# Attention values with the value rows stationary, the probabilities normalised before their transposes, and attention steps in the order scores, transposes, values

## The chip, the cores and the metric

The kernel runs on one core of one Trainium2 chip. The metric is the device time of one execution in microseconds (us), the median of several runs. A core has a matrix engine (PE, its weight loads are shown as PEld), a vector engine (DVE), a scalar engine (ACT), a general engine (POOL) and a queue processor that starts transfers (SP). They run in parallel, each through its own list of instructions in order, and wait for one another through semaphores.

## What is computed

One decoder layer over 256 tokens of width 1024, in float32. Of it the change touches the attention (8 heads of width 64; with 256 tokens there is one block, so the selected blocks are all masked out and causal attention over the own block is left) and the depthwise convolution:

```python
def reference(x, ...):
    h = rmsnorm(x, g_mix[l])
    proj = h @ w_in[l]                       # q, k, v, u (convolution), two gates
    o = moba_attention(q, k, v)              # softmax(q k^T / 8, causal) v, per head
    branch_a = o.reshape(b, s, ATTN_WIDTH) @ w_attn_up[l]
    z = a * jax.nn.sigmoid(g)                # a, g: the halves of u
    z = conv(z, w_dw) + b_dw                 # 31 taps, causal, per channel (512 channels)
    cz = silu(layernorm(z, ln_g, ln_b))
    branch_c = cz @ w_conv_pw[l] + b_conv_pw[l]
    x = x + (gate_a * branch_a + gate_c * branch_c) @ w_out[l]
    h = rmsnorm(x, g_ffn[l])
    x = x + jnp.square(jax.nn.relu(h @ w_ff1[l])) @ w_ff2[l]
    return rmsnorm(x, g_final)
```

## The kernel before

Every large product is computed in split precision: a weight block `raw` (128 x 4 x 512) is split into `w_hi` (a cast on ACT, `high(n)`, L386) and `w_lo` (a subtraction on DVE, `low(n)`, L558), the activations likewise into `a_hi`, `a_lo`, and three matmuls (L811, L812, L815) take the place of one. The work goes in **units**, numbered n: one unit is 4 blocks of rows times 2 token tiles times 3 matmuls of 512 columns, 24 in all. Units 0 to 17 are the input projection, two units to an output block of 512 columns (b = n // 2), which goes to PSUM banks 0 and 1 or 2 and 3 in turn and is taken out by ACT in `take(b)` (L423). So unit 14, the first of block 7, cannot start before `take(5)` has emptied its banks (semaphore `evac`). Units 18 to 25 are the two branches and the output projection, then follow the feed-forward units and a loop over them.

The steps of the attention and of the convolution stand between these units, written out by hand: the loop over n says for each engine what it does at **step n**. Each engine keeps to this order, and a step that waits holds up all that stands behind it on its engine. Weights are prepared three units ahead: step n has `high(n + 3)` first on ACT and `low(n + 3)` on DVE.

Attention goes by pairs of heads, p = 0 to 3, and starts at `S_ATT` = 9. A pair passes through these pieces:

- `scores(p)` on PE, step 9 + p (L873 with the two heads in the upper and the lower 64 rows of the array, L876 adds the causal mask by a matmul with an identity), to banks 6 and 7. It covers 256 query rows as s = 1 (256 keys) and s = 0 (128 keys).
- `row_max(p)` on DVE, same step (L602, L604, L607), then `exps(p)` on ACT (L434, L437), which also sums the rows.
- `probs_transposed(p)` on PE, step 10 + p: six transposes (L798) to banks 4 and 5, copied out by `probs_out(p)` on ACT (L447).
- `values(p)` on PE, step 11 + p (L903): the transposed probabilities are the stationary operand (128 x 128) and 64 columns of `v_nat` the moving one, six float32 matmuls, each of which the trace shows as two. The result goes to banks 6 and 7, columns 384 to 511, beside the next scores.
- `inverse(p)` (L611) and `o_out(p)` (L618) on DVE: the result times the inverse row sums, to `o_nat`, tokens on partitions.
- at step 15 (`S_OT`) eight transposes of `o_nat` on PE (L798), split on ACT and DVE to `b_hi` and `b_lo` (L481, L650).

On PE a step has the order unit, values(n - 11), probs_transposed(n - 10), scores(n - 9). Since scores and values share banks, `scores(p)` waits for `o_made` of the values before:

```python
if p >= 2:
    pe.wait_ge(o_made, p - 1)
```

The convolution is 31 taps for 4 channel blocks, 124 instructions on DVE over z (tap 0: L591, others: L596), dealt out by the table `CONV_AT` as the last piece of steps 2 to 14, after `low(n + 3)`. Step 16 (`S_LN`) has the transposes of the result and the layer norm. At step 13 (`S_BIAS`) ACT splits the bias rows, and POOL then subtracts (L368).

## Time and profile before

| what | us |
|---|---|
| median of 3 runs | 365.58 (365.08 to 365.93) |
| the profiled execution | 366.68 |
| its span on the core | 364.7 |
| PE busy | 353.4 (97% of the span) |
| DVE busy | 256.2 (70%) |
| ACT busy | 174.8 (48%) |

The span is the time from the first to the last instruction of the profiled execution; the time of that execution is 2.0 us more, which lies around it. Matmuls are pipelined, and the end of one is modelled: a matmul of 512 columns is shown with 0.39 us while the next starts 0.23 us after it. So lengths of work on PE are best read as differences of starts.

### The profile page before, as it was taken

To read this page: it belongs to the slowest core of one execution; us is meant where nothing else is said; L and a number is where in the kernel's file an instruction comes from. 1 tells how busy PE (TensorE), PEld (TensorE's weight loads), DVE (VectorE), ACT (ScalarE), POOL (GpSimd) and SP (SyncE) were. 2 spreads that over 40 slices of the span, in tenths; PEclk is the share of its full clock that TensorE was granted. 3 is DMA by queue.
4 is the path that set the end of the run, shared out by engine and by line. 5 is a ranking of instruction groups with operands and counts; after the bars stand their busy time and mean duration, and the time that the engine had idled before them with its cause. 6 is when DMAs were issued, how large, how long until landed. Compare 5 with 4: busy or idle time off the path is not lost.

```text
span 364.7 us, 4601 instructions
## 1 busy us (share of the span) xinstructions
PE 353.4 (97%) x1760; PEld 292.7 (80%) x1760; DVE 256.2 (70%) x314; ACT 174.8 (48%) x195; POOL 9.2 (3%) x18
## 2 busy tenths in 40 slices
PE   6899999999999999999999999999999999999993
PEld 3688888777788888888888888888888888888882
DVE  0878999898899879993858663747636485463834
ACT  3694545554494646342545643436344263541513
POOL 3000000000012000000000000000000000000000
PEclk9899999999999999999999999999999999999999
DMA  7999374633333463757354493571837628260003
GB/s 269 336 345 324 119 229 132 216 117 115 117 115 116 146 238 136 243 188 261 117 152 157 159 328 130 189 259 35 321 115 226 234 67 279 113 230 0 0 0 115
DMA packets 33993, 63.71 MB, mean 175 GB/s; under 512 B 1178, under 2 KB 5434, under 8 KB 33980
## 3 DMA queue, kind: packets, MB, share of 16 engines
q1 hardware_dynamic: 33676, 63.01, 51.4%
q10 hardware_dynamic: 304, 0.53, 0.4%
q8 instruction: 9, 0.15, 0.2%
q14 instruction: 4, 0.03, 0.0%
HBM read 62.48 MB, written 1.05 MB: 174 GB/s over the span
## 4 chain that ended last, share of the span: by engine, by line
PE 89%; DVE 5%; issue 2%; DMA 2%; ACT 0%; SPq 0%; POOLq 0%; POOL 0%
PE ps L815 20%; PE ps L811 20%; PE ps L812 20%; PE ps L1013 16%; PE ps L1015 8%; PE ps L798 3%; DVE conv L596 2%; DMA raw<-in_w_in_dram 2%; DVE w_lo L558 1%; PE ps L873 1%; PE ps L903 1%; PE ps L876 1%; DVE smax L602 0%; DVE w_lo L575 0%; PE ps L987 0%
## 5 line engine op out<-in xcount | busy, mean ns | idle before, releaser
L811 PE MATMUL ps<-w_hi,a_lo 128*128 128x512 f32 x288 | 114.4, 397 | 3.0 <-DVE a_lo L570 3.0
L815 PE MATMUL ps<-w_lo,a_hi 128*128 128x512 f32 x288 | 113.0, 392 | 0.3 <-DVE w_lo L575 0.3
L812 PE MATMUL ps<-w_hi,a_hi 128*128 128x512 f32 x288 | 112.9, 392 | 0.0
L1013 PE MATMUL ps<-b_both,w_hi 128*128 128x512 f32 x256 | 90.8, 399 | 0.0
L1015 PE MATMUL ps<-b_both,w_lo 128*128 128x256 f32 x256 | 71.9, 281 | 0.0
L386 ACT CAST w_hi<-raw 128x2048 fp32r<-128x2048 f32 (+1 forms) x30 | 56.4, 1884 | 31.3 <-PE ps L815 26.9
L558 DVE TENSOR_TENSOR w_lo<-raw,w_hi 128x2048 fp32r<-128x2048 f32 x29 | 66.1, 2285 | 4.7 <-ACT w_hi L386 4.6
L762 DVE TENSOR_TENSOR w_lo<-raw,w_hi 128x2048 fp32r<-128x2048 f32 x28 | 63.5, 2289 | 6.4 <-ACT w_hi L532 6.4
L811 PEld LDWEIGHTS ps<-w_hi,a_lo 128*128 128x128 f32 x288 | 54.5, 189 | 14.2 <-DVE w_hi L564 3.2
L815 PEld LDWEIGHTS ps<-w_lo,a_hi 128*128 128x128 f32 x288 | 54.5, 189 | 12.5 <-DVE w_lo L575 0.8
L812 PEld LDWEIGHTS ps<-w_hi,a_hi 128*128 128x128 f32 x288 | 54.5, 189 | 10.7
L1013 PEld LDWEIGHTS ps<-b_both,w_hi 128*128 128x128 f32 x256 | 48.1, 188 | 11.9
L532 ACT CAST w_hi<-raw 128x2048 fp32r<-128x2048 f32 x28 | 52.8, 1911 | 7.8 <-PE ps L815 7.8
L596 DVE SCALAR_TENSOR_TENSOR conv<-z,dw,conv 128x256 f32<-128x256 f32 x120 | 50.8, 499 | 0.0
L1015 PEld LDWEIGHTS ps<-b_both,w_lo 128*128 128x128 f32 x256 | 48.3, 189 | 0.3
L741 DVE TENSOR_TENSOR nat<-ps,nat 128x512 f32<-128x512 f32 x16 | 11.1, 692 | 42.5 <-ACT nat L516 42.5
L516 ACT COPY nat<-ps 128x512 f32<-128x512 f32 x16 | 9.4, 588 | 57.5 <-PE ps L1015 57.5
L811 PE MATMUL ps<-w_hi,b_both 128*128 128x512 f32 x48 | 18.9, 393 | 0.0
L815 PE MATMUL ps<-w_lo,b_both 128*128 128x512 f32 x48 | 18.7, 390 | 0.0
L812 PE MATMUL ps<-w_hi,b_both 128*128 128x512 f32 x48 | 18.7, 389 | 0.0
L754 DVE TENSOR_TENSOR a_lo<-nat,a_hi 128x1024 fp32r<-128x1024 f32 x7 | 8.6, 1223 | 14.1 <-ACT a_hi L522 14.1
L522 ACT CAST a_hi<-nat 128x1024 fp32r<-128x1024 f32 x7 | 7.4, 1052 | 21.8 <-PE ps L815 21.6
(109 smaller groups left out, 218.8 us busy)
## 6 DMA issues: line engine op xcount, KB each, us to landing
raw<-in_w_ff_dram SPq DMA_DIRECT2D x32, 1024.0 KB, 5.4
raw<-in_w_in_dram SPq DMA_DIRECT2D x14, 1024.0 KB, 5.3
raw<-in_w_out_dram SPq DMA_DIRECT2D x4, 1024.0 KB, 5.0
raw<-in_w_in_dram SPq DMA_DIRECT2D x6, 512.0 KB, 7.5
raw<-in_w_attn_up_dram SPq DMA_DIRECT2D x2, 1024.0 KB, 5.1
raw<-in_w_conv_pw_dram SPq DMA_DIRECT2D x2, 1024.0 KB, 5.1
res<-in_x_dram SPq DMA_DIRECT2D x2, 512.0 KB, 3.7
raw<-in_w_in_dram SPq DMA_DIRECT2D x4, 256.0 KB, 5.9
```

The lines of the kernel that those rows point to most:

```text
L386: nc.scalar.copy(w_hi[:, n % SLOTS, part], raw[:, n % SLOTS, part]).then_inc(hi_made, 1)
L532: nc.scalar.copy(w_hi[:, slot], raw[:, slot]).then_inc(hi_made, 1)
L558: nc.vector.tensor_tensor(w_lo[:, n % SLOTS], raw[:, n % SLOTS], w_hi[:, n % SLOTS].bitcast(F32), ALU.subtract).then_inc(lo_made, 1)
L596: nc.vector.scalar_tensor_tensor(out=conv[:, c], in0=z[:, c, tap:tap + T], scalar=dw[:, w:w + 1], in1=conv[:, c], op0=ALU.mult, op1=ALU.ad ...
L741: nc.vector.tensor_tensor(hid[:, pair], ps[:, TB + 2 * half:TB + 2 * half + 2, 0:T], hid[:, pair], ALU.add).then_inc(sum_made, 1)
L762: nc.vector.tensor_tensor(w_lo[:, slot], raw[:, slot], w_hi[:, slot].bitcast(F32), ALU.subtract).then_inc(lo_made, 1)
L798: return nc.tensor.transpose(dst, src, ident[0:src.shape[0], 0:src.shape[0]])
L811: nc.tensor.matmul(dst, lo[:, tok], w_hi[:, slot, k], start=start, stop=False)
L812: nc.tensor.matmul(dst, hi[:, tok], w_hi[:, slot, k], start=False, stop=False)
L815: return nc.tensor.matmul(dst, hi[:, tok], w_lo[:, slot, k], start=False, stop=stop)
L1013: nc.tensor.matmul(ps[:, TB + c], w_hi[:, slot, k, cols], b_both[:, kk].rearrange("p a t -> p (a t)"), start=kk == 0, stop=False)
L1015: last = nc.tensor.matmul(ps[:, TB + c, 0:T], w_lo[:, slot, k, cols], b_hi[:, kk], start=False, stop=kk == KD - 1)
```

## The change

The values are computed the other way round: 64 columns of `v_nat` are stationary, and the transposed probabilities move (256 columns for the first 128 keys, 128 for the others; the first 128 queries have no others). The two heads of a pair write to the lower and the upper 64 partitions of one half bank (bank 5, columns 256 to 511), with channels on partitions, which is what the next product needs: the eight transposes of step 15 go, and `o_nat` becomes `o_t`. As the row sums then no longer lie on the partitions, the probabilities are normalised ahead of their transposes, by four instructions on ACT (`normalise`), for which `inverse(p)` moves one step forward on DVE, to behind `low(n + 3)`. `o_out` becomes a copy on ACT. The mask matmul of s = 1 covers only the 128 keys that need it. On PE a step has the order unit, scores, transposes, values; `scores(p)` waits for the exponentials of the pair before and no longer for the values. Tap 0 of the convolution goes to ACT (4 instructions, steps 2 and 4), and `CONV_AT` gives DVE 11 or 12 taps in steps 9 to 12, where it had 10, and 9 and 1 in steps 13 and 14, where it had 10 and 9. The bias split moves to step 14.

```diff
 S_QT, S_KT = 6, 8
 S_ATT = 9
 PAIRS = HEADS // 2
-S_OT = S_ATT + 6
-S_BIAS = 13
+S_OLO = S_ATT + 6
+S_BIAS = 14
 S_LN = 16
 S_SILU = U_ATTN
 
 
-CONV = [(tap, c) for tap in range(10) for c in (0, 1)]
-CONV += [(tap, c) for tap in range(10) for c in (2, 3)]
+CONV = [(tap, c) for tap in range(1, 10) for c in (0, 1)]
+CONV += [(tap, c) for tap in range(1, 10) for c in (2, 3)]
 CONV += [(tap, c) for tap in range(10, TAPS) for c in range(4)]
-CONV_AT = {2: 6, 3: 14, 4: 9, 5: 9, 6: 9, 7: 9, 8: 9, 9: 10, 10: 10, 11: 10, 12: 10, 13: 10, 14: 9}
-assert len(CONV) == sum(CONV_AT.values()) == TAPS * 4
+CONV_AT = {2: 6, 3: 12, 4: 9, 5: 9, 6: 9, 7: 9, 8: 9, 9: 11, 10: 12, 11: 12, 12: 12, 13: 9, 14: 1}
+assert len(CONV) == sum(CONV_AT.values()) == (TAPS - 1) * 4
 
...
+            def normalise(p):
+
+                act.wait_ge(rinv_made, p + 1)
+                act.wait_ge(exp_made, p + 1)
+                for h in range(2):
+                    part = probs[:, 256 * h:256 * h + 256]
+                    nc.scalar.activation(part, part, ACT.Copy, scale=rinv[:, p, h:h + 1])
+                for h in range(2):
+                    part = probs[:, 512 + 128 * h:640 + 128 * h]
+                    last = nc.scalar.activation(part, part, ACT.Copy, scale=rinv[:, p, 2 + h:3 + h])
+                last.then_inc(norm_made, 1)
+
+            def o_out(p):
+
+                act.wait_ge(pv_done, p + 1)
+                nc.scalar.copy(o_t[:, p], o_pair()).then_inc(ot_made, 1)
+
...
@@ -459,6 +481,12 @@
                         act.wait_ge(glu_tr, c + 1)
                         nc.scalar.activation(conv[:, c], ps[:, TB + c, T:2 * T], ACT.Sigmoid,
                                              bias=vec[:, V_BGLU + CC + c:V_BGLU + CC + c + 1]).then_inc(glu_sig, 1)
+                    act.wait_ge(vec_made, 2)
+                    act.wait_ge(const_made, 4)
+                    for c in (2 * GLU_AT[n], 2 * GLU_AT[n] + 1):
+                        act.wait_ge(z_made, c + 1)
+                        nc.scalar.activation(conv[:, c], z[:, c, 0:T], ACT.Identity, scale=dw[:, c:c + 1],
+                                             bias=vec[:, V_BDW + c:V_BDW + c + 1]).then_inc(conv_first, 1)
...
+                if S_ATT + 2 <= n < S_ATT + 2 + PAIRS:
+                    o_out(n - S_ATT - 2)
                 if S_ATT + 1 <= n <= S_ATT + PAIRS:
                     probs_out(n - S_ATT - 1)
                 if S_ATT <= n < S_ATT + PAIRS:
                     exps(n - S_ATT)
+                    normalise(n - S_ATT)
...
-                if n == S_OT:
-                    act.wait_ge(o_tr, 1)
-                    nc.scalar.copy(b_hi[:, 0:CC], chunks(TB)).then_inc(o_hi, 1)
+                if n == S_OLO:
+                    act.wait_ge(ot_made, PAIRS)
+                    nc.scalar.copy(b_hi[:, 0:CC], o_t[:]).then_inc(o_hi, 1)
...
                 for m in conv_share(step):
                     tap, c = CONV[m]
-                    if tap == 0:
-                        nc.vector.tensor_scalar(conv[:, c], z[:, c, 0:T], dw[:, c:c + 1], vec[:, V_BDW + c:V_BDW + c + 1],
-                                                ALU.mult, ALU.add).then_inc(conv_step, 1)
+                    if tap == 1:
+                        dve.wait_ge(conv_first, c + 1)
                     else:
                         dve.wait_ge(conv_step, conv_before(m) + 1)
-                        w = tap * CC + c
-                        nc.vector.scalar_tensor_tensor(out=conv[:, c], in0=z[:, c, tap:tap + T], scalar=dw[:, w:w + 1],
-                                                       in1=conv[:, c], op0=ALU.mult, op1=ALU.add).then_inc(conv_step, 1)
+                    w = tap * CC + c
+                    nc.vector.scalar_tensor_tensor(out=conv[:, c], in0=z[:, c, tap:tap + T], scalar=dw[:, w:w + 1],
+                                                   in1=conv[:, c], op0=ALU.mult, op1=ALU.add).then_inc(conv_step, 1)
...
             def inverse(p):
                 dve.wait_ge(exp_made, p + 1)
                 nc.vector.reciprocal(rinv[:, p], psums[:, p]).then_inc(rinv_made, 1)
-
-            def o_out(p):
-
-                dve.wait_ge(pv_done, p + 1)
-                dve.wait_ge(rinv_made, p + 1)
-                for s in range(2):
-                    last = nc.vector.tensor_tensor(
-                        o_nat[:, 1 - s, 128 * p:128 * p + 128].rearrange("p (h d) -> p h d", h=2),
-                        ps[:, SB0:SB0 + 2, 384 + HD * s:384 + HD * s + HD],
-                        rinv[:, p, 2 * s:2 * s + 2].rearrange("p (h a) -> p h a", a=1).to_broadcast([P, 2, HD]), ALU.mult)
-                last.then_inc(o_made, 1)
...
-                if S_ATT + 2 <= n < S_ATT + 2 + PAIRS:
-                    o_out(n - S_ATT - 2)
-                if S_ATT + 1 <= n < S_ATT + 1 + PAIRS:
-                    inverse(n - S_ATT - 1)
                 if S_ATT <= n < S_ATT + PAIRS:
                     row_max(n - S_ATT)
-                if n == S_OT:
-                    dve.wait_ge(o_hi, 1)
-                    nc.vector.tensor_tensor(b_lo[:, 0:CC], chunks(TB), b_hi[:, 0:CC].bitcast(F32),
-                                            ALU.subtract).then_inc(o_lo, 1)
...
                 if n + AHEAD < U_LOOP + AHEAD_LOOP:
                     low(n + AHEAD)
+                if S_ATT <= n < S_ATT + PAIRS:
+                    inverse(n - S_ATT)
                 conv_products(n)
+                if n == S_OLO:
+                    dve.wait_ge(o_hi, 1)
+                    nc.vector.tensor_tensor(b_lo[:, 0:CC], o_t[:], b_hi[:, 0:CC].bitcast(F32),
+                                            ALU.subtract).then_inc(o_lo, 1)
...
             def scores(p):
 
-
-
-                if p >= 2:
-                    pe.wait_ge(o_made, p - 1)
                 for s, at, keys in ((1, 0, 256), (0, 256, 128)):
...
                     for h in range(2):
-                        last = nc.tensor.matmul(ps[:, SB0 + h, at:at + keys], ident_b[:], mask_b[:, T - keys:T],
+                        last = nc.tensor.matmul(ps[:, SB0 + h, at + keys - P:at + keys], ident_b[:], mask_b[:, P:T],
                                                 start=False, stop=True)
...
             def probs_transposed(p):
-                pe.wait_ge(exp_made, p + 1)
+                pe.wait_ge(norm_made, p + 1)
                 if p:
                     pe.wait_ge(pt_made, p)
-                for blk in range(6):
-                    o = blk * P
-                    last = transpose(ps[:, TB + o // W, o % W:o % W + P], probs[:, o:o + P])
+                if p > 1:
+                    pe.wait_ge(ot_made, p - 1)
+                for h in range(2):
+                    for blk, at in enumerate((512 + P * h, 256 * h, 256 * h + P)):
+                        o = (3 * h + blk) * P
+                        last = transpose(ps[:, TB + o // W, o % W:o % W + P], probs[:, at:at + P])
                 last.then_inc(p_tr, 1)
 
             def values(p):
 
                 pe.wait_ge(pt_made, p + 1)
                 if p:
-                    pe.wait_ge(o_made, p)
-                if p + 2 <= PAIRS:
-                    pe.wait_ge(exp_made, p + 2)
-                for s in range(2):
+                    pe.wait_ge(ot_made, p)
+                for kb in range(2):
                     for h in range(2):
                         head = slice(HD * (2 * p + h), HD * (2 * p + h) + HD)
-                        o = 384 + HD * s
-                        n_keys = 2 - s
-                        for kb in range(n_keys):
-                            at = 256 * h + P * kb if s == 0 else 512 + P * h
-                            last = nc.tensor.matmul(ps[:, SB0 + h, o:o + HD], probs_t[:, at:at + P], v_nat[:, kb, head],
-                                                    start=kb == 0, stop=kb == n_keys - 1)
+                        at = 3 * h * P + 2 * P * kb
+                        last = nc.tensor.matmul(o_pair()[HD * h:HD * h + HD, kb * P:T], v_nat[:, kb, head],
+                                                probs_t[:, at:at + T - kb * P], start=kb == 0, stop=kb == 1)
                 last.then_inc(pv_done, 1)
 
             def glu_transposed(hb):
@@ -933,24 +944,23 @@
                 if n == S_KT:
                     pe.wait_ge(evac, K + 1)
                     transpose_chunks(SB0, lambda t, c: nat[:, t, W + c * P:W + c * P + P]).then_inc(qk_tr, 1)
+                if S_ATT <= n < S_ATT + PAIRS:
+                    if n == S_ATT:
+                        pe.wait_ge(qk_made, 2)
+                        pe.wait_ge(ident_made, 3)
+                    else:
+                        pe.wait_ge(exp_made, n - S_ATT)
+                    scores(n - S_ATT)
+                if S_ATT + 1 <= n <= S_ATT + PAIRS:
+                    probs_transposed(n - S_ATT - 1)
                 if S_ATT + 2 <= n < S_ATT + 2 + PAIRS:
                     if n == S_ATT + 2:
                         pe.wait_ge(evac, V + 1)
                     values(n - S_ATT - 2)
-                if S_ATT + 1 <= n <= S_ATT + PAIRS:
-                    probs_transposed(n - S_ATT - 1)
-                if S_ATT <= n < S_ATT + PAIRS:
-                    if n == S_ATT:
-                        pe.wait_ge(qk_made, 2)
-                        pe.wait_ge(ident_made, 3)
-                    scores(n - S_ATT)
-                if n == S_OT:
-                    pe.wait_ge(o_made, PAIRS)
-                    transpose_chunks(TB, lambda t, c: o_nat[:, t, c * P:c * P + P]).then_inc(o_tr, 1)
...
-                    pe.wait_ge(conv_step, TAPS * CC)
-                    pe.wait_ge(o_lo, 1)
+                    pe.wait_ge(conv_step, (TAPS - 1) * CC)
+                    pe.wait_ge(ot_made, PAIRS)
```

On **PE**, step 12 (behind unit 12) stands before:

```order
L903 MATMUL ps<-v_nat,probs_t 128x64 x6
L798 MATMUL ps<-ident,probs 128x128 x6
L873 MATMUL ps<-qk_t 128x256 x2
L876 MATMUL ps<-mask_b,ident_b 128x256 x2
L873 MATMUL ps<-qk_t 128x128 x2
L876 MATMUL ps<-mask_b,ident_b 128x128 x2
L811 MATMUL ps<-w_hi,a_lo 128x512
```

and step 12 now:

```order
L886 MATMUL ps<-qk_t 128x256 x2
L889 MATMUL ps<-mask_b,ident_b 128x128 x2
L886 MATMUL ps<-qk_t 128x128 x2
L889 MATMUL ps<-mask_b,ident_b 128x128 x2
L815 MATMUL ps<-ident,probs 128x128 x6
L914 MATMUL ps<-probs_t,v_nat 64x256 x2
L914 MATMUL ps<-probs_t,v_nat 64x128 x2
L828 MATMUL ps<-w_hi,a_lo 128x512
```

The rows ahead of the last, which is the start of unit 13, are the pieces of pairs 1 to 3. Values moved from the front to the back, from six matmuls of 64 columns to two of 256 and two of 128 (the 64 is the width of the stationary operand), and the first mask has 128 columns in place of 256.

On **ACT**, from the exponentials of pair 3 (step 12) to the cast of unit 16's weights, stands before:

```order
L434 ACTIVATE probs,psums<-ps,nbias 128x256 x2
L437 ACTIVATE probs,psums<-ps,nbias 128x128 x2
L423 ACT_TABLE_LOAD
L423 ACTIVATE gates<-ps,rstd 128x512 x2
L386 CAST w_hi<-raw 128x2048
L468 CAST bias_rows<-gfin_bc 128x1024
```

and now:

```order
L439 ACTIVATE probs,psums<-ps,nbias 128x256 x2
L442 ACTIVATE probs,psums<-ps,nbias 128x128 x2
L453 ACTIVATE probs<-probs,rinv 128x256 x2
L456 ACTIVATE probs<-probs,rinv 128x128 x2
L428 ACT_TABLE_LOAD
L428 ACTIVATE gates<-ps,rstd 128x512 x2
L391 CAST w_hi<-raw 128x2048
L462 COPY o_t<-ps 128x256
L469 COPY probs_t<-ps 128x768
```

Four multiplications (`probs<-probs,rinv`) moved in ahead of the table load and of `take(5)` (`gates<-ps,rstd`), the copy of the values stands ahead of `probs_out(3)`, and the bias rows have gone from here.

On **DVE**, step 12 stands before:

```order
L618 TENSOR_TENSOR o_nat<-ps,rinv 128x128 x2
L611 RECIPROCAL rinv<-psums 128x4
L602 TENSOR_REDUCE smax<-ps 128x2
L604 TENSOR_REDUCE smax<-ps 128x2
L607 TENSOR_SCALAR nbias<-smax 128x4
L558 TENSOR_TENSOR w_lo<-raw,w_hi 128x2048
L596 SCALAR_TENSOR_TENSOR conv<-z,dw,conv 128x256 x10
```

and now:

```order
L632 TENSOR_REDUCE smax<-ps 128x2
L634 TENSOR_REDUCE smax<-ps 128x2
L637 TENSOR_SCALAR nbias<-smax 128x4
L589 TENSOR_TENSOR w_lo<-raw,w_hi 128x2048
L641 RECIPROCAL rinv<-psums 128x4
L626 SCALAR_TENSOR_TENSOR conv<-z,dw,conv 128x256 x12
```

The copy of the values is gone, the reciprocal moved from ahead of the row maxima to behind the subtraction `w_lo`, now for the pair of the same step, and 12 taps stand where 10 stood.

## Rows read from the trace of the kernel before

**Rows 1.** The page, part 1 (busy time, instructions) and part 4 (chain that ended last).

```profile
PE 353.4 (97%) x1760; PEld 292.7 (80%) x1760; DVE 256.2 (70%) x314; ACT 174.8 (48%) x195; POOL 9.2 (3%) x18
PE 89%; DVE 5%; issue 2%; DMA 2%; ACT 0%; SPq 0%; POOLq 0%; POOL 0%
```

**Rows 2.** Windows: length, busy of PE, PEld, DVE, ACT, POOL, clock, DMA.

```profile
60.00:130.00 70.00, 69.22 (x374) 56.28 (x374) 62.24 (x118) 39.20 (x61) 4.63 (x2) 1.00 0.42 140
200.00:300.00 100.00, 100.00 (x502) 84.50 (x501) 58.74 (x39) 44.98 (x33) 0.00 (x0) 1.00 0.57 187
```

**Rows 3.** Timeline of PE, step 12: start, length, what, [idle before <-releaser].

```profile
95.15 0.39 PE L815 MATMUL ps<-w_lo,a_hi 128*128 128x512 f32 x1
95.38 1.44 PE L903 MATMUL ps<-v_nat,probs_t 128*128 128x64 f32 x12
96.66 0.82 PE L798 MATMUL ps<-ident,probs 128*128 128x128 f32 x6
97.87 0.70 PE L873 MATMUL ps<-qk_t 64*128 64x256 f32 x4 [0.39 <-DVE o_nat L618]
98.51 0.39 PE L876 MATMUL ps<-mask_b,ident_b 128*128 128x256 bf16 x2
98.83 0.49 PE L873 MATMUL ps<-qk_t 64*128 64x128 f32 x4
99.25 0.29 PE L876 MATMUL ps<-mask_b,ident_b 128*128 128x128 bf16 x2
99.35 0.48 PE L811 MATMUL ps<-w_hi,a_lo 128*128 128x512 f32 x1
```

**Rows 4.** Timeline of PE: values of pair 2, its next transposes, unit 14.

```profile
104.89 1.45 PE L903 MATMUL ps<-v_nat,probs_t 128*128 128x64 f32 x12
106.17 0.82 PE L798 MATMUL ps<-ident,probs 128*128 128x128 f32 x6
106.75 0.47 PE L811 MATMUL ps<-w_hi,a_lo 128*128 128x512 f32 x1
```

**Rows 5.** Timeline of PE: output transposes of step 15, unit 16.

```profile
119.14 1.04 PE L798 MATMUL ps<-ident,o_nat 128*128 128x128 f32 x8
119.93 0.47 PE L811 MATMUL ps<-w_hi,a_lo 128*128 128x512 f32 x1
```

**Rows 6.** Groups by line and form: count, then busy us, mean ns, idle before.

```profile
L876 PE MATMUL ps<-mask_b,ident_b 128*128 128x256 bf16 x8 | 1.6, 278 | 0.0
L876 PE MATMUL ps<-mask_b,ident_b 128*128 128x128 bf16 x8 | 1.1, 224 | 0.0
L434 ACT ACTIVATE probs<-ps,nbias 128x256 f32<-128x256 f32 x8 | 3.7, 471 | 7.4 <-DVE nbias L607 7.4
L437 ACT ACTIVATE probs<-ps,nbias 128x128 f32<-128x128 f32 x8 | 2.9, 368 | 0.0
L548 ACT ACTIVATE res<-gates,rstd 128x512 f32<-128x512 f32 x2 | 1.4, 724 | 1.7 <-POOL rstd L363 1.7
```

**Rows 7.** Timeline of DVE, step 12 and the taps of step 13.

```profile
99.58 0.69 DVE L602 TENSOR_REDUCE smax<-ps 128x2 f32<-128x512 f32 x1 [1.68 <-PE ps L876]
100.71 2.28 DVE L558 TENSOR_TENSOR w_lo<-raw,w_hi 128x2048 fp32r<-128x2048 f32 x1
102.91 4.04 DVE L596 SCALAR_TENSOR_TENSOR conv<-z,dw,conv 128x256 f32<-128x256 f32 x10
106.87 0.48 DVE L618 TENSOR_TENSOR o_nat<-ps,rinv 128x128 f32<-128x128 f32 x2
109.53 6.20 DVE L596 SCALAR_TENSOR_TENSOR conv<-z,dw,conv 128x256 f32<-128x256 f32 x10
```

**Rows 8.** Timeline of ACT, step 12: first exponential, table load, `take(5)`.

```profile
100.84 0.48 ACT L434 ACTIVATE probs<-ps,nbias 128x256 f32<-128x256 f32 x1 [2.52 <-DVE nbias L607]
102.57 1.28 ACT L423 ACT_TABLE_LOAD   x1
105.03 1.90 ACT L386 CAST w_hi<-raw 128x2048 fp32r<-128x2048 f32 x1
```

More of the change, by code:

```diff
@@ L81, in conv_before @@
     tap, c = CONV[m]
-    return CONV.index((tap - 1, c))
+    return CONV.index((tap - 1, c)) if tap > 1 else None
 def build(nc, x, g_mix, w_in, b_glu, w_dw, b_dw, ln_g, ln_b, w_conv_pw, b_conv_pw,
@@ L225, in build @@
         z_made = sem("z_made")
+        conv_first = sem("conv_first")
         conv_step = sem("conv_step")
@@ L245, in build @@
         rinv_made = sem("rinv_made")
-        o_made = sem("o_made")
-        o_tr = sem("o_tr")
+        norm_made = sem("norm_made")
+        ot_made = sem("ot_made")
         o_hi = sem("o_hi")
```

12 lines of the change are left out of this document (7 added, 5 removed).

## The prediction

> **What bounds the kernel now.** The page comes first: PE is busy for 353.4 of 364.7 us, and the chain that ended last runs 89% over PE [rows 1]. Then the windows: in the stretch that holds the attention, 60 to 130, PE is busy for 69.22 of 70 us and DVE for 62.24, and in the feed-forward stretch 200 to 300 PE is busy for 100 of 100 [rows 2]. So PE is the bound everywhere from 60 on, and what the change is worth is the PE time it takes out between the units, less every wait that it brings in. What comes later has no idle PE time that could swallow a gain (it depends on PE, and moves forward with it), so a gain at unit 17 is a gain at the end. DVE, at 89% of the attention stretch, is the engine to watch: the change also moves work there. Third, the timeline of PE at step 12, which is the model for steps 11 and 12 [rows 3]: the last matmul of unit 12 starts at 95.15 and holds PE for 0.23, then values take 1.28 (95.38 to 96.66), transposes and a wait 1.21 (to 97.87), scores 1.48 (to 99.35). All that is 3.97 between two units. A unit is 5.54 (99.35 to the next values at 104.89) [rows 3, 4].
>
> **The four gains on PE.** I take each from differences of starts.
>
> Output transposes: the eight of step 15 take 0.79 (119.14 to 119.93) [rows 5]. They go, and nothing takes their place on PE: **0.79**.
>
> Masks: eight mask matmuls of 256 columns become 128 wide. Mean lengths are 278 and 224 ns [rows 6], so 8 x 0.054 = **0.43**. Scores then take 1.48 - 0.11 = 1.37.
>
> Waits: six transposes alone take 0.58 (106.17 to 106.75) [rows 4], or 0.10 each by the eight above, so of the 1.21 about 0.60 is work and 0.61 is the wait of the scores for `o_made`; the view's idle column has 0.39, because ends are modelled [rows 3]. Step 11 has the same wait. The new scores wait for exponentials that are long done (below), so 2 x 0.6 = **1.2**, with 0.8 as the low end.
>
> Values: now 12 instructions in 1.28 [rows 3]. The new form isn't in this trace; the nearest rows are the scores, where the two heads also share the array, by rows in place of columns. There the 256-column pair takes 0.64 (97.87 to 98.51) and the 128-column pair 0.42 (98.83 to 99.25), each as four shown matmuls. The difference, 0.22 for two passes that do 128 columns less, gives 0.11 for a pass of 128 and 0.22 for one of 256, if both heads run at once, and an overhead of 0.20 for entering and leaving. (In turn, the 256-column pair would need at least 4 x 0.22 = 0.88, and it took 0.64, so for scores they do run at once.) New values are one such pair of 256 and one of 128, next to each other: 0.44 + 0.22 + 0.20 = 0.86. If the overhead is paid twice, 1.06; with none, 0.66. If heads in different columns run in turn, 4 x 0.22 + 4 x 0.11 + 0.20 = 1.52. I take 0.90, near the one-overhead value, since nothing else stands between the two pairs: 4 x (1.28 - 0.90) = **1.52**, with ends of 4 x (1.28 - 0.66) = 2.5 and 4 x (1.28 - 1.52) = -0.96.
>
> The trace shows two heads at once only for row halves. The Trainium skill (TensorEngine Tiling (Array Packing), Performance Considerations) advises just this swap for 64 columns, with two column tiles, for a factor of up to 2; the same page says under Tiling Modes that a change of mode drains the engine, which speaks against one more kind of matmul in each step. The first rule would put the values at the 0.86 above in place of 1.52; for the second the 0.20 of the score rows is the price, already in.
>
> Sum of the gains: 0.79 + 0.43 + 1.2 + 1.52 = **3.94**.
>
> **What the change adds, and who waits.** I set a clock to zero at the end of the scores of pair 0, the start of unit 10, and add rows.
>
> PE: unit 10 to 5.54; scores and transposes 1.97, so unit 11 from 7.51 to 13.05; scores, transposes, values 2.87, so unit 12 from 15.92 to 21.46; again 2.87, so unit 13 from 24.33 to 29.87; transposes and values 1.50, so PE wants unit 14 at **31.37**.
>
> DVE: the maxima start 0.23 behind the end of the scores (99.58 against 99.35) [rows 3, 7]. A step is maxima 1.13, `low` 2.20, reciprocal 0.1, and taps at 0.396 (10 in 102.91 to 106.87) [rows 7]: 7.79 with 11 taps, 8.18 with 12. So the maxima of pairs 1, 2, 3 start at 8.02, 16.20, 24.38. Their scores are done at 6.9, 14.4 and 22.8: it is now the taps that make DVE late, by about 1.3. In rows 7 DVE had 1.68 idle in their place. At 8.18 against PE's 8.41 per step the lag doesn't grow.
>
> ACT: exponentials start 1.26 behind the maxima (99.58 to 100.84) and take 1.6 [rows 7, 8]. The normalisation waits for the reciprocal, which stands behind `low`: 3.33 + 0.2 after the maxima. Its price, from both sides: ACT reading SBUF with a scale from a tile took 724 ns for 512 columns, and 128 columns are worth 0.10 (471 - 368) [rows 6], so 0.52 and 0.42; ACT instructions follow one another 0.1 before the shown end, so 2 x 0.42 + 2 x 0.32 = 1.48. If SBUF cost nothing over PSUM it would be 1.3; I keep 1.9 as the high end.
>
> Now each wait. Scores of pair 3 (21.46) need the exponentials of pair 2: 16.20 + 2.9 + 0.1 = 19.2, in time. Transposes of pair 2 (22.83) need its normalisation: 16.20 + 3.53 + 1.48 + 0.1 = 21.3, in time. Transposes of pair 3 (29.87): 24.38 + 5.11 = 29.5, in time by 0.4. **Unit 14** needs `take(5)`, which stands behind the normalisation of pair 3: 29.4, then table load and evacuation 2.46 (102.57 to 105.03) [rows 8], so 31.85, and 0.1 for the signal: 31.95, against 31.37. PE waits **0.6**. Before, `take(5)` ended at 105.03, 1.7 before unit 14 (106.75) [rows 4, 8]; this cover is gone. With normalisation at 1.3 the wait is 0.4, at 1.9 it is 1.0 (part of it ahead of the transposes).
>
> Edits at no cost: four first taps on ACT (about 1.1 in each of steps 2 and 4) and the copy of the values (0.3 to 0.4) lie in ACT's slack (ACT busy 48% [rows 1]), and what they delay is a weight cast prepared three units ahead. The moved bias split makes POOL work beside `low(17)` instead of beside taps. It was there that ten taps took 6.20 and not 4.04 [rows 7], so DVE may lose 2.2 in step 14 too. But after the maxima of pair 3 it has left 12, 9 and 1 taps and two `low`: 24.38 + 8.18 + 2.2 + 3.6 + 2.2 + 2.2 + 0.4 = 43.2, and PE wants the last tap only at the end of unit 16, at 31.95 + 3 x 5.54 + 0.9 = 49.5. Each wait instruction more is some tens of ns on a sequencer that runs ahead.
>
> **Forecast.** 3.94 - 0.6 = 3.3 to 3.4. I take 3.4: the profiled execution of 366.68 (span 364.7 and 2.0 around it) would become 363.3 (span 361.3). That execution was 1.1 above the median, so the median of 365.58 becomes **362.2**.
>
> **Rivals.**
> (a) The two heads run in turn, so the change of form doesn't do what it should. Then values take 1.52. The gain is 0.79 + 0.43 + 1.2 - 0.96 = 1.46, and the wait at unit 14 is gone, since PE comes 1.9 later than in the sum above: **364.1**. For it: the trace has no column halves. Against it: the row halves do run at once. In between (half overlapped, 1.1 to 1.2): gain 2.6 to 2.9.
> (b) DVE becomes the bound in steps 10 to 12, mildly: taps at 0.50 instead of 0.396 make its step 9.4 against 8.4, the lag grows by 1.0 a step, and the waits take 3.0 of the 3.9: gain 0.9, and at 0.52 nothing measurable is left: **365.2**.
> (c) The other side: the taps run at 0.62, as the ten from 109.53 did [rows 7]. If ACT's normalisation from SBUF to SBUF slows them as POOL's work did there, a DVE step is 10.9 against 8.4. The spare time of exponentials (2.2) and transposes (1.5 and 0.4) is used up in the first such step; PE then waits 0.45 and 0.8 in step 12, about 3.9 before the transposes of pair 3 and 1.0 before unit 14, some 6.1 in all, against 3.94 gained: 2.1 slower, **367.7**. It decides from about 0.54 a tap. Against it: casts from SBUF to SBUF on ACT stand in this stretch too, and the taps beside the one at 105.03 are among the ten of 4.04 [rows 7, 8].
>
> **How the numbers follow.** Forecast, with values of 0.7 to 1.1 and a wait of 0.3 to 1.2 (gain 2.8 to 3.9): 0.68. (a), with half overlaps down to a gain of 1.2: 0.21. (b), within 0.2%: 0.06. (c): 0.04; a cause I haven't seen gives the last 0.01. A measurement of this kernel can tell about 0.2%, 0.7 us. The range goes from 361.3 (gain of 3.9 and 0.4 for scatter) to 364.4 (case (a) and 0.3 of scatter). Faster 0.90, same 0.06, slower 0.04.
>
> **What the profile after would show.** Right: unit 12 to unit 13 (start to start) 8.4 instead of 9.5; two new value groups of 256 and 128 columns with start pairs a few ns apart, 0.9 in all; no idle before the scores; unit 15 to unit 16 without transposes, 5.5 instead of 6.3; DVE maxima starting 1 to 1.6 behind the scores, with no idle before them; one wait of about 0.6 at unit 14, released by `take(5)`. Wrong: value matmuls of the two heads each starting when the other ends (a); taps of over 0.45, and waits of transposes for the normalisation in steps 11 to 13 (b, c); a wait at unit 16 or 17, or a feed-forward stretch in which PE is less than fully busy, where I count on none.

## The result and the profile after

| | before | after |
|---|---|---|
| median | 365.62 us (365.08 to 366.34, 6 runs) | 362.38 us (361.91 to 363.14, 6 runs) |
| the profiled execution | 366.68 | 362.36 |
| its span | 364.7 | 360.4 |

The ratio of the times is 0.9911, with a 95% interval from 0.99 to 0.9921: 3.2 us faster, where 3.4 were forecast.

The page of after, its parts 1 and 4, answers to [rows 1]. PE is busy 3.8 us less at the same 97%, and ACT 9.1 us more.

```profile
PE 349.6 (97%) x1736; PEld 287.0 (80%) x1736; DVE 253.2 (70%) x302; ACT 183.9 (51%) x219; POOL 10.6 (3%) x18
...
PE 90%; ACT 2%; DMA 2%; issue 2%; SPq 2%; DVE 0%; POOLq 0%; POOL 0%; ACTq 0%
```

The windows answer to [rows 2] (length, busy of PE, PEld, DVE, ACT, POOL, clock, DMA share, GB/s).

```profile
60.00:130.00 70.00, 70.00 (x366) 54.68 (x365) 63.17 (x110) 47.68 (x82) 6.07 (x2) 1.00 0.42 143
200.00:300.00 100.00, 100.00 (x500) 84.50 (x499) 59.71 (x37) 44.46 (x32) 0.00 (x0) 1.00 0.57 189
```

The view shows no idle time of PE between 60 and 130 any more, and the feed-forward stretch is as full as before. So the gain of the attention steps went through to the end.

The timeline of PE at step 12 answers to [rows 3].

```profile
93.14 0.39 PE L832 MATMUL ps<-w_lo,a_hi 128*128 128x512 f32 x1
93.45 0.70 PE L886 MATMUL ps<-qk_t 64*128 64x256 f32 x4
94.09 0.29 PE L889 MATMUL ps<-mask_b,ident_b 128*128 128x128 bf16 x2
94.31 0.49 PE L886 MATMUL ps<-qk_t 64*128 64x128 f32 x4
94.73 0.29 PE L889 MATMUL ps<-mask_b,ident_b 128*128 128x128 bf16 x2
94.85 0.82 PE L815 MATMUL ps<-ident,probs 128*128 128x128 f32 x6
95.61 0.87 PE L914 MATMUL ps<-probs_t,v_nat 128*64 128x256 f32 x8
96.41 0.50 PE L828 MATMUL ps<-w_hi,a_lo 128*128 128x512 f32 x1
96.74 0.39 PE L829 MATMUL ps<-w_hi,a_hi 128*128 128x512 f32 x1
```

Nothing waits. Scores take 1.40 (93.45 to 94.85), transposes 0.76, values 0.80. One row is not what it was: the last matmul of unit 12 holds PE for 0.31 (93.14 to 93.45), not 0.23. And unit 13's first takes 0.33 (96.41 to 96.74). These edges come back below.

The length of a step, from the first matmul of its unit to the first of the next, follows from such rows (step 12: 87.77 to 96.41 after). In us:

| step | 9 | 10 | 11 | 12 | 13 | 14 | 15 | 16 | sum |
|---|---|---|---|---|---|---|---|---|---|
| before | 7.11 | 7.79 | 9.54 | 9.54 | 7.40 | 6.81 | 6.37 | 6.33 | 60.89 |
| after | 7.00 | 7.63 | 8.58 | 8.63 | 7.18 | 6.48 | 5.61 | 6.23 | 57.35 |
| gain | 0.11 | 0.16 | 0.96 | 0.91 | 0.22 | 0.33 | 0.76 | 0.10 | 3.54 |
| predicted | 0.11 | 0.11 | 1.10 | 1.10 | -0.22 | 0.38 | 0.79 | 0 | 3.4 |

From the start of unit 17 to that of unit 25 it is 47.25 us before and 47.26 after. The two profiled executions differ by a further 0.8 us ahead of unit 9 (it starts at 65.37 and at 64.56). The edits of steps 2 to 4 aren't the cause: over all the kernels of this study unit 9 starts between 64.04 and 65.69, at 64.11 in the one that has the new steps 9 to 16 with the taps of before, and the medians don't show this part.

The same starts can be summed by kind of work over steps 9 to 16, which closes the account: the values fell from 5.10 to 3.24 (1.86), the scores with their masks from 5.91 to 5.56 (0.35), the transposes with the waits behind them from 5.34 to 3.62 (1.72), and the matmuls of the units rose from 44.54 to 44.92 (-0.38). That is 3.55.

### The profile page after: what moved, and what is told of

Its sections match the earlier page's. It is cut to its first block, busy times and chain, and to the rows that moved or that the text cites. A ratio compares the mean times of both kernels' runs of the same rounds, so it can differ in the third digit from the quotient of the medians.

```text
span 360.4 us, 4567 instructions
## 1 busy us (share of the span) xinstructions
PE 349.6 (97%) x1736; PEld 287.0 (80%) x1736; DVE 253.2 (70%) x302; ACT 183.9 (51%) x219; POOL 10.6 (3%) x18
## 4 chain that ended last, share of the span: by engine, by line
PE 90%; ACT 2%; DMA 2%; issue 2%; SPq 2%; DVE 0%; POOLq 0%; POOL 0%; ACTq 0%
PE ps L828 20%; PE ps L832 19%; PE ps L829 19%; PE ps L1023 17%; PE ps L1025 8%; PE ps L815 3%; DMA raw<-in_w_in_dram 2%; PE ps L886 1%; ACT w_hi L391 1%; SPq L301 1%; PE ps L914 1%; SPq L316 1%; PE ps L889 0%; ACT nat L410 0%; ACT nat L428 0%
```

## The experiments

"Steps" below means the sum of steps 9 to 16 as in this table. The kernels ran on three chips in three groups, with before beside each group at 365.73, 365.72 and 365.71.

**Do the two heads of the values run at once? Two runs.** In after the two heads' matmuls alternate. The first run groups them by head; the second starts from the first.

```diff
-                for kb in range(2):
-                    for h in range(2):
+                for h in range(2):
+                    for kb in range(2):
```

> The kernel after, with one edit: the loops of the values are exchanged, so that each head has its 256-column and its 128-column matmul in a row, and only then comes the other head. In the kernel after the group of values takes 0.80 us (start to the next unit). Theory A, the two column halves run at once because matmuls of different heads stand next to each other: now they meet only at the border, the group takes 1.3 to 1.5, the kernel is 4 x 0.6 = 2.0 to 2.8 us slower (364.4 to 365.2), and the small wait at unit 14 stays small. Rival B, the order within the group does not matter, since the engine overlaps what it may, or since the short time of the group has another cause than overlap: 0.8 as before, no change within 0.3 us.

It took 362.15 (361.92 to 362.43), ratio 0.9902 [0.9885, 0.9919], steps 57.40: B was right and my theory A wrong. The timeline of PE between 86.46 and 86.50 shows why:

```profile
86.45 0.44 PE L914 MATMUL ps<-probs_t,v_nat 128*64 128x256 f32 x2
```

Within 0.05 us two matmuls of 256 columns have started. Each head has one of these, which the trace shows as two, and head 1's is issued after all of head 0's, those of 128 columns too. So the two column halves are fed out of the order of the program (the second run shows below that the pair isn't the two parts of one head's matmul), and the order inside the group is worth nothing. That leaves open whether they run at once because of the halves. Second run:

```diff
-o_pair()[HD * h:HD * h + HD, kb * P:T]
+o_pair()[0:HD, kb * P:T]
```

> The kernel with the values grouped by head (as in e1_heads_apart, 0.81 us for the group), in which both heads write to the same 64 output partitions, so the upper half of the values is not computed and the lower one holds only the second head. Same number and size of matmuls. Theory A, the 0.80 us are two heads at once in different column halves, whatever order they are issued in: in one half they run in turn, the group takes 4 x 0.22 + 4 x 0.11 + 0.2 or a little less, 1.35 to 1.5, and the kernel is 4 x 0.6 = 2.2 to 2.8 us slower than e1 (364.4 to 364.9), with starts of the two heads no longer in pairs. Rival B, 64-column stationary operands are simply that fast: 0.8, no change.

It took 364.83 (364.19 to 367.18), ratio 0.9978 [0.9956, 0.9999], steps 59.80: 2.40 over the first run, 0.6 in each step with values. Both heads now write the lower 64 partitions, and the upper half of the values isn't computed. The group of values, of the first run and then of this one:

```profile
86.45 0.88 PE L914 MATMUL ps<-probs_t,v_nat 128*64 128x256 f32 x8
```

```profile
87.58 1.51 PE L914 MATMUL ps<-probs_t,v_nat 128*64 128x256 f32 x8
```

And the timeline of this run between 87.59 and 87.63:

```profile
87.58 0.43 PE L914 MATMUL ps<-probs_t,v_nat 128*64 128x256 f32 x1
```

Same instructions, 0.63 longer, and of 256 columns only one starts in the same 0.05 us. The concurrency of the halves is 2.4 us of this kernel: without it the kernel would have taken about 364.8, 0.7 above rival (a)'s 364.1. One thing stays open: in this run the two heads share their destination as well as their half, and the runs don't tell which of the two makes them take turns.

**What is the order worth, without the new form?** Before, with the order scores, transposes, values on PE, and ACT and DVE doing their parts in the order that this needs. The values keep their old form and go to bank 5. The edit on PE:

```diff
-                    values(n - S_ATT - 2)
...
                     scores(n - S_ATT)
...
                     probs_transposed(n - S_ATT - 1)
...
+                    values(n - S_ATT - 2)
```

> The kernel before with the order of the steps alone: scores, transposes, values on PE, and values in their old form (six matmuls of 64 columns) but written to bank 5, so that scores need not wait for them. DVE copies them out behind its weight subtraction, ACT copies the transposes behind the exponentials. Masks, taps, output transposes as before. Theory A, of the 3.2 us of the whole change about 0.9 is the wait that the order removes: transposes and wait were 1.21 in steps 11 and 12 and become 0.75, twice 0.46, less 0.17 in step 13, so 0.6 to 1.1 us faster than before (364.5 to 365.0), with no idle PE time ahead of the scores. Rival B, the order gives nothing alone, since transposes or values then wait for the slower copy on DVE: within 0.3 us of before, and new waits at transposes or values.

It took 364.9 (364.44 to 365.16), ratio 0.9975 [0.9964, 0.9986], steps 59.99, 0.90 less: A. Steps 11 and 12 gave 0.49 and 0.45, step 10 gave 0.06, and steps 13 and 14 took 0.11 back. No row of its timeline of PE has an idle column in these steps. Of step 12:

```profile
95.80 0.82 PE L800 MATMUL ps<-ident,probs 128*128 128x128 f32 x6
96.46 1.45 PE L903 MATMUL ps<-v_nat,probs_t 128*128 128x64 f32 x12
```

The transposes take 0.66 here. So the wait taken out was worth about 0.45 a step, in two steps, and not 0.6. The trace of before could have told this: its step 10 has the same two groups with no wait between them, and there the transposes ahead of scores take 0.75, so of the 1.21 of step 12 only 0.46 was a wait.

```profile
78.04 0.81 PE L798 MATMUL ps<-ident,probs 128*128 128x128 f32 x6
78.79 0.70 PE L873 MATMUL ps<-qk_t 64*128 64x256 f32 x4
```

**The narrower mask alone.**

```diff
-last = nc.tensor.matmul(ps[:, SB0 + h, at:at + keys], ident_b[:], mask_b[:, T - keys:T],
+last = nc.tensor.matmul(ps[:, SB0 + h, at + keys - P:at + keys], ident_b[:], mask_b[:, P:T],
```

> The kernel before with one edit: the mask matmul of s = 1 covers 128 keys and not 256. Theory A (the scores of after take 1.40 and those of before 1.48, so 0.08 a step): steps 9 to 12 each 0.08 shorter, 0.32 in all, ratio 0.9991. The prediction's term (lengths of the two forms, 0.054 a matmul): 0.11 a step, 0.43 in all. Rival B: the bf16 mask matmuls hide behind the score matmuls, and the 0.08 of after comes from what stands around the scores there: nothing in steps 9 and 10, and steps 11 and 12 unchanged too.

Steps 9 to 12 took 7.00, 7.68, 9.43 and 9.43, each 0.11 less, 0.43 in all; 365.31 (364.8 to 365.7), ratio 0.9988 [0.9979, 0.9997]. The prediction's term was right to the hundredth, and my revision of it to 0.32 wrong. Its timeline:

```profile
96.71 0.70 PE L873 MATMUL ps<-qk_t 64*128 64x256 f32 x4 [0.38 <-DVE o_nat L618]
...
97.98 0.29 PE L876 MATMUL ps<-mask_b,ident_b 128*128 128x128 bf16 x2
98.08 0.48 PE L811 MATMUL ps<-w_hi,a_lo 128*128 128x512 f32 x1
```

Scores take 1.37 (96.71 to 98.08), as predicted. The 1.40 of after has 0.03 more behind its masks (94.73 to 94.85 against 97.98 to 98.08), where transposes follow and not a unit: an edge again.

**Fewer changes of the array's shape.** The two masks of a head are merged into one of 384 columns, put first, and the row halves of the scores follow without a break. (The mask tile grows to 384 columns; that part of the edit isn't shown.)

```diff
+                for h in range(2):
+                    nc.tensor.matmul(ps[:, SB0 + h, 0:384], ident_b[:], mask_b[:], start=True, stop=False)
                 for s, at, keys in ((1, 0, 256), (0, 256, 128)):
...
-                    for h in range(2):
-                        last = nc.tensor.matmul(ps[:, SB0 + h, at + keys - P:at + keys], ident_b[:], mask_b[:, P:T],
```

> The kernel after with the masks of a head as one matmul of 384 columns (zeros, triangle, triangle) ahead of both score matmuls, which then accumulate onto it: one entry to the 64-row form per pair instead of two. Theory A on the price of an entry: the group of scores falls from 1.40 to 1.15 to 1.25 us (0.20 less for an entry, 0.11 more mask columns, weight loads of the masks hidden behind the unit). Theory B on what of it arrives: the maxima of pair 3 hang on the taps and not on the scores, so only the saving of pair 0 (0.2) moves take(5), and unit 14 now waits 0.5 to 0.6: the kernel gains only 0.2 to 0.3 (362.1). Rival, nothing hangs on DVE's chain: the whole 0.6 to 0.9 arrives (361.6), and unit 14 does not wait.

It took 361.81 (361.61 to 362.04), ratio 0.9892 [0.9876, 0.9909], steps 56.96: 0.39 less than after, in between what was expected. Steps 9 to 12 gained 0.18, 0.10, 0.15 and 0.15, at and below the low end of the 0.15 to 0.25 expected, and step 13 lost 0.21 to a wait. Its timeline of PE at step 12, and then unit 14:

```profile
92.56 0.50 PE L886 MATMUL ps<-mask_b,ident_b 128*128 128x384 bf16 x2
92.99 0.92 PE L890 MATMUL ps<-qk_t 64*128 64x256 f32 x8
93.84 0.87 PE L817 MATMUL ps<-ident,probs 128*128 128x128 f32 x6
94.64 0.87 PE L915 MATMUL ps<-probs_t,v_nat 128*64 128x256 f32 x8
...
102.84 0.50 PE L830 MATMUL ps<-w_hi,a_lo 128*128 128x512 f32 x1 [0.18 <-ACT gates L430]
```

Masks and scores take 1.28 (92.56 to 93.84) and the transposes 0.80. The matmul of unit 12 ahead of the masks, which use the full array, takes 0.23 again and not 0.31. PE comes to unit 14 earlier, and `take(5)` is late there, as the prediction had reckoned for after itself.

**The convolution's shares, four runs.** More taps in steps 10 to 12, so that DVE is later behind the scores:

```diff
-9: 11, 10: 12, 11: 12, 12: 12, 13: 9, 14: 1}
+9: 11, 10: 14, 11: 14, 12: 14, 13: 3, 14: 1}
```

> The kernel after with 14 taps in place of 12 in steps 10, 11 and 12 and 3 in place of 9 in step 13 (120 in all). Theory A, DVE is late by the taps, and the chain maxima, exponentials, reciprocal, normalisation, table load, take(5) is just in time for unit 14 (a wait of 0.04): two steps with two more taps each move the maxima of pair 3 by 4 x 0.395 = 1.6 us, and all of it arrives: about 0.6 ahead of the transposes of pair 3 and 0.9 ahead of unit 14, the kernel 1.4 to 1.7 us slower (363.8 to 364.1). Rival B, the chain has slack that the trace does not show or the taps merely fill DVE's idle time: slower by less than 0.5.

It took 363.61 (363.52 to 363.71), ratio 0.994 [0.9924, 0.9957], a little below A's 363.8 to 364.1. Only step 13 grew, from 7.18 to 8.67, by 1.49 where 1.4 to 1.7 were expected:

```profile
102.14 0.87 PE L815 MATMUL ps<-ident,probs 128*128 128x128 f32 x6 [0.34 <-ACT probs L456]
...
104.72 0.50 PE L828 MATMUL ps<-w_hi,a_lo 128*128 128x512 f32 x1 [0.90 <-ACT gates L428]
```

This is the chain of rivals (b) and (c): DVE late, normalisation late, then transposes and `take(5)`. It is real and decides where the prediction put it, in step 13. Now the shares of before, with the first tap still on ACT (the same table was then put on the kernel with the mask first), and then with all 124 taps on DVE (table and first taps then as in before). The edit of the first of these two:

```diff
-9: 11, 10: 12, 11: 12, 12: 12, 13: 9, 14: 1}
+9: 10, 10: 10, 11: 10, 12: 10, 13: 10, 14: 7}
```

> The kernel after with 10 taps in each of steps 9 to 13 and 7 in step 14 (120 in all), as the steps had before. Theory A, the chain over DVE and ACT is just in time with 12 taps, so with fewer it comes early and PE, which waited only 0.04, gains nothing: within 0.2 us of the kernel after (362.1 to 362.5), DVE idle ahead of the maxima again by 1 to 1.7 us, take(5) ending 1.3 to 2 earlier relative to unit 14. The larger shares then are no part of the gain. Rival B, the larger shares are worth something, since 10 and 7 taps in steps 13 and 14, where POOL slows them, make the taps late for step 16: 0.5 or more slower, with PE waiting ahead of the convolution's transposes.

> After, with the first tap back on DVE and the convolution shares of before (124 taps on DVE, none on ACT). Theory A (first taps on ACT and the larger shares are no part of the gain, since DVE is late behind the scores only by what the waits can spare): the length of after within 0.2, steps 9 to 13 within 0.05 of it, unit 14 with a wait of at most 0.1. Rival B (ACT's help is needed): the four taps more on DVE make it late in steps 13 to 16, and unit 16 or 17 waits 0.5 to 1.6 for conv or w_lo.

They took 362.03 (361.99 to 362.74), ratio 0.9903 [0.9885, 0.9921], and 362.29 (361.8 to 362.82), ratio 0.9912 [0.9897, 0.9927], with steps 57.34 and 57.37 against 57.35. Neither the larger shares nor ACT's taps are a part of the gain. But one thing expected of the first didn't come: `take(5)` was to end 1.3 to 2 us earlier against unit 14. DVE's maxima of pair 3 do start earlier, 1.35 ahead of unit 13 (94.79 against 96.14) where after has 0.58 (95.83 against 96.41), yet the table load starts 4.56 behind unit 13 in both. Two rows of its timelines, of ACT and of DVE, show why:

```profile
96.26 0.37 ACT L462 COPY o_t<-ps 128x256 f32<-128x256 f32 x1 [2.39 <-PE ps L914]
98.98 0.18 DVE L641 RECIPROCAL rinv<-psums 128x4 f32<-128x4 f32 x1 [0.77 <-ACT probs L442]
```

On ACT the exponentials of pair 3 stand behind the copies of the values and of the transposes, and these wait for PE's values of the same step. So a second chain leads to `take(5)`, which starts at PE's values and moves with PE. It leaves unit 14 a wait of 0.04 (the group of values ahead of it takes 0.84, the other groups 0.80), however early DVE is. In after the chain over DVE's taps and `w_lo` ends together with it, at the reciprocal of pair 3 (99.25); with 14 taps it ends later, and decides. The shares matter only where PE comes to unit 14 earlier:

> Both together: masks of 384 columns first (e4_mask_first, which saved 0.15 to 0.18 a step and lost 0.21 of it again at unit 14) and 10 taps a step. Theory A, the 0.21 at unit 14 was DVE's lag by the taps: it goes, and steps 9 to 13 are each 0.10 to 0.18 shorter than in the kernel after, 0.6 in all over steps 9 to 16, 361.6 us, 0.2 faster than e4_mask_first. Rival B, the wait at unit 14 has another cause (the table load and take(5) alone): it stays at 0.2 and the kernel equals e4_mask_first (361.8).

It took 361.36 (361.31 to 362.93), ratio 0.9879 [0.9862, 0.9895], steps 56.80. The wait at unit 14 is back at the 0.04 of after (step 13 is 7.18 and not 7.39, step 14 gives 0.05 back), and this kernel has the lowest median of the study, though its interval overlaps that of the mask first alone.

**The other order with the new form, two runs.** After, with the order values, transposes, scores. As the result of the values shares a bank with the transposes, these then wait for ACT's copy `o_t`.

```diff
+                    values(n - S_ATT - 2)
...
                     probs_transposed(n - S_ATT - 1)
...
-                    values(n - S_ATT - 2)
...
             def probs_transposed(p):
-                if p > 1:
-                    pe.wait_ge(ot_made, p - 1)
+                if p:
+                    pe.wait_ge(ot_made, p)
```

> The kernel after with the steps on PE in the old order values, transposes, scores. Values and transposes share bank 5, so the transposes have to wait for the copy of the values just done (in the kernel after that copy has a whole unit of time). Theory A, the order is worth a bank wait per step in the new form too: 0.6 to 0.8 ahead of the transposes in steps 11, 12 and 13, and up to 0.3 at unit 14, together 1.9 to 2.6 us slower than the kernel after (364.2 to 364.9). Rival B, the order does not matter once values have left the banks of the scores: within 0.3 us of the kernel after.

It took 369.67 (369.17 to 370.37), ratio 1.0102 [1.0082, 1.0122], steps 64.54: 7.2 more than after, where 1.9 to 2.6 were expected. I had missed what stands ahead of the copy on ACT. Timeline of PE, the transposes of steps 12 and 13, and unit 14:

```profile
97.13 0.85 PE L815 MATMUL ps<-ident,probs 128*128 128x128 f32 x6 [0.97 <-ACT o_t L462]
...
109.33 0.85 PE L815 MATMUL ps<-ident,probs 128*128 128x128 f32 x6 [3.55 <-ACT o_t L462]
...
110.75 0.63 PE L828 MATMUL ps<-w_hi,a_lo 128*128 128x512 f32 x1
111.18 0.63 PE L829 MATMUL ps<-w_hi,a_hi 128*128 128x512 f32 x1
```

And its timeline of ACT ahead of the second of these waits:

```profile
104.57 1.28 ACT L428 ACT_TABLE_LOAD   x1
105.86 1.26 ACT L428 ACTIVATE gates<-ps,rstd 128x512 f32<-128x512 f32 x2
107.02 1.90 ACT L391 CAST w_hi<-raw 128x2048 fp32r<-128x2048 f32 x1
108.81 0.38 ACT L462 COPY o_t<-ps 128x256 f32<-128x256 f32 x1
```

The values were issued at 104.91, and their copy stood behind a table load, `take(5)` and a weight cast until 108.81. Behind the 3.55 us of idle PE the clock fell, though not at once: PE worked for 1.4 us at the upper level first (its transposes and three matmuls of unit 14), and from 110.75 on matmuls of 512 columns start 0.43 apart and not 0.23. The windows give 0.66 as the granted clock of that stretch (second last columns: clock, then DMA share):

```profile
105.00:110.00 5.00, 1.45 (x15) 1.09 (x15) 3.79 (x8) 4.18 (x5) 0.00 (x0) 1.00 0.48 186
110.00:115.00 5.00, 5.00 (x17) 3.97 (x16) 5.00 (x11) 4.70 (x5) 0.01 (x1) 0.66 0.42 156
```

That is a part of the stretch at the lower of the two levels (1.2 GHz) and the rest at the upper (2.4 GHz). Step 14 took 8.07 for it and not 6.48, another 1.6 us. To tell ACT's queue from the order itself, ACT then copies first:

```diff
+                if S_ATT + 2 <= n < S_ATT + 2 + PAIRS:
+                    o_out(n - S_ATT - 2)
                 if n + AHEAD < U_LOOP + AHEAD_LOOP:
                     high(n + AHEAD)
...
-                if S_ATT + 2 <= n < S_ATT + 2 + PAIRS:
-                    o_out(n - S_ATT - 2)
```

> After with the PE order of before (values, transposes, scores; transposes wait for the copy of the values), as in e6_old_order, but ACT copies the values ahead of the weight cast, not behind it. Theory A (the 7.2 us lost in e6_old_order are waits for a copy queued behind casts on ACT, plus a fall of the clock behind the longest): PE idle about 0.7 in steps 11 and 12 and 1.7 to 1.9 in step 13, no fall of the clock, 3.1 to 3.3 slower than after, about 365.4. Rival B (the order and the shared bank cost this in themselves, whatever ACT's order): as e6_old_order, 369 to 370.

It took 365.15 (364.67 to 366.03), ratio 0.9985 [0.9976, 0.9995], steps 60.29, 2.94 more than after: A, a little below its 3.1 to 3.3. The waits:

```profile
95.08 0.85 PE L815 MATMUL ps<-ident,probs 128*128 128x128 f32 x6 [0.56 <-ACT o_t L462]
...
105.48 0.85 PE L815 MATMUL ps<-ident,probs 128*128 128x128 f32 x6 [1.72 <-ACT o_t L462]
106.08 0.48 PE L828 MATMUL ps<-w_hi,a_lo 128*128 128x512 f32 x1
106.40 0.40 PE L829 MATMUL ps<-w_hi,a_hi 128*128 128x512 f32 x1
```

After 1.72 idle the clock stays up: the matmuls behind 106.40 start 0.23 apart. So 4.3 of the 7.2 were the place of one copy on ACT (waits and clock), and 2.9 the order with a shared bank.

## Why the prediction was right, and where its steps were off

The bound was right: PE, from 60 on, and each gain went through to the end. Of the sum:

**Output transposes**, 0.79: step 15 gave 0.76, and unit 16 another 0.10 that wasn't in the sum. Behind the eight transposes its first matmul held PE for 0.32; now it follows unit 15 directly and takes 0.23 (115.68 to 115.91). Rows of PE's timeline of after, against [rows 5]:

```profile
115.68 0.39 PE L828 MATMUL ps<-w_hi,a_lo 128*128 128x512 f32 x1
115.91 0.39 PE L829 MATMUL ps<-w_hi,a_hi 128*128 128x512 f32 x1
```

**Masks**, 0.43: measured alone, 0.43.

**Values**, 0.90 taken, 0.80 measured (95.61 to 96.41, and 109.27 to 110.07): 4 x 0.48 = 1.92 and not 1.52. The reasoning from the row halves held: both heads at once and one overhead gave 0.86, and heads in turn gave 1.52, where the run with both in one half has 1.44. The first passes of the two heads start within 0.01 us in after (86.97 to 86.98).

The advice of the Trainium skill (TensorEngine Tiling (Array Packing), Performance Considerations) to swap the operands for 64 columns and use two column tiles, which the prediction weighed, agrees with the group's sizes here: 0.80 in two halves, 0.63 more in one.

**Waits**, 1.2 taken, about 0.9 measured. This is the mis-sized term. The step that failed reads "six transposes alone take 0.58", so that about 0.60 of the 1.21 is work. That 0.58 was a group with a unit behind it. With values behind it, it takes 0.75 (timeline of after):

```profile
102.00 0.82 PE L815 MATMUL ps<-ident,probs 128*128 128x128 f32 x6
102.75 0.87 PE L914 MATMUL ps<-probs_t,v_nat 128*64 128x256 f32 x8
```

With scores behind it, it takes 0.75 too, and with the old values behind it 0.66. So what follows starts later, most of all where it uses halves of the array; the old values use the whole of it, so a change of shape isn't all of the price. The idle column of [rows 3], 0.39, was closer to the truth than the 0.61 that I put in its place; 0.46 is what remained. The prediction had put the price of a change of the array's shape inside the group, as its 0.20. A part of it lies in the neighbours: 0.08 in the last matmul of a unit ahead of scores or new values (0.31 against 0.23) and 0.17 in the transposes ahead of either (0.75 against 0.58). The first matmul of a unit takes 0.31 behind any small group, halves or not, against 0.23 behind another unit, and 0.33 behind the new values. With the values coming out 0.1 cheaper, steps 11 and 12 gave 0.96 and 0.91, not 1.10.

**Unit 14**, a wait of 0.6 taken, 0.04 measured; this cost term was the largest single miss. ACT's side came out right in time: its timeline in step 12 has

```profile
99.46 0.91 ACT L453 ACTIVATE probs<-probs,rinv 128x256 f32<-128x256 f32 x2 [0.24 <-DVE rinv L641]
...
100.97 1.28 ACT L428 ACT_TABLE_LOAD   x1
102.27 1.26 ACT L428 ACTIVATE gates<-ps,rstd 128x512 f32<-128x512 f32 x2
103.42 1.90 ACT L391 CAST w_hi<-raw 128x2048 fp32r<-128x2048 f32 x1
```

1.51 for the normalisation (99.46 to 100.97, 1.48 reckoned) and 2.45 for load and evacuation. The exponentials started 1.65 behind the maxima (97.48 against 95.83) and not 1.26, for the reason that the run with 10 taps showed; the prediction had left ACT's copies out. It cost nothing, since the subtraction `w_lo` on DVE ended no sooner. But PE came later than on my clock. Steps 10 to 13 without waits were reckoned at 7.51, 8.41, 8.41 and 7.04 and took 7.63, 8.58, 8.63 and 7.14, 0.6 more in all, which is these edges. The same error took 0.4 out of the gains of these steps (2.29 for 2.69) and took away the wait of 0.6, so the sum of 3.4 stands close to the 3.54 by errors that cancel, which is luck. The experiment with the mask first, where PE comes 0.4 earlier, has the wait (0.18 in its idle column), which is what the mechanism says.

**DVE** ran as reckoned: the maxima of pairs 2 and 3 start 8.14 apart, 8.18 reckoned, with 12 taps in 4.80:

```profile
87.69 0.69 DVE L632 TENSOR_REDUCE smax<-ps 128x2 f32<-128x512 f32 x1
...
91.11 4.80 DVE L626 SCALAR_TENSOR_TENSOR conv<-z,dw,conv 128x256 f32<-128x256 f32 x12
95.83 0.68 DVE L632 TENSOR_REDUCE smax<-ps 128x2 f32<-128x512 f32 x1
```

So ACT's normalisation doesn't slow the taps, which rivals (b) and (c) needed (0.50 and 0.62 a tap; it is 0.40). The 0.62 was a misreading of [rows 7]: the ten taps of 6.20 are one of 2.63 and nine at 0.40 each, as the timeline of before shows when it is cut at 111.9:

```profile
109.53 2.63 DVE L596 SCALAR_TENSOR_TENSOR conv<-z,dw,conv 128x256 f32<-128x256 f32 x1
```

That one tap ends 0.3 behind POOL's subtraction of the bias rows (107.95 to 111.88, where POOL's times are rough), while `w_lo` beside the same subtraction took its usual 2.26. The one tap of step 14 in after, beside the end of that subtraction, took 2.61; two taps beside its start (110.34 and 110.74) took 0.40. Why the one is held isn't shown. So POOL costs one tap some 2.2 us, as the prediction allowed for in step 14, and doesn't slow all taps, as (c) had it. Nobody waits for it.

**The rivals.** (a) was the serious one, and the run with both heads in one half shows its price, 2.4 us in the steps and 2.7 in the medians. The prediction had 4 x (1.52 - 0.90) = 2.5 for it, of which the wait at unit 14 was to give 0.6 back; as that wait wasn't there, nothing came back. No run has the new form of the values in the old order without a shared bank, so the form and the order are priced together with the neighbours, as above.

## What to carry to other kernels

Price a small group on PE by the starts of its neighbours too: here a group in halves of the array cost 0.08 us in the matmul ahead of it (0.17 where that was a group of transposes), any small group cost 0.08 in the first matmul behind it, and a group taken out or merged gives it back (0.10 behind the removed transposes, 0.10 to 0.18 a step for the merged masks). Swapping a narrow moving operand for a narrow stationary one with two column halves is worth it where two such products are independent. Before a wait is moved to another engine's result, read what stands ahead of that result in its engine's queue: one copy behind a cast and a table load cost more here than the whole change gained.

## What the runs showed of the chip

Two column halves of the array don't keep the order of the program between them: a matmul issued after two others to the other half started within 0.05 us of the first of them, and both orders take the same 0.80 to 0.81 us for the group. With both heads in one half, one alone started in such 0.05 us, and the group took 1.44.

In one kernel PE, busy until then, was idle for 3.55 us and worked for 1.4 us at the upper clock, and then matmuls of 512 columns started 0.43 apart from 110.75 to 113.74, at the lower clock. In the same kernel with the copy moved, 1.72 us idle in the same place was followed by the usual 0.23.

Beside POOL's subtraction of 1 x 1024 one tap of the convolution on DVE took 2.6 us in place of 0.40 and ended about 0.3 behind POOL, before and after; the subtraction `w_lo` on DVE beside it kept its 2.3 us.
